# Output weights two groups of value pages later in SyncE's queue, and one value step moved from round 7 to round 58, in a mixed attention decode kernel

## The reference, cut to what matters

```python
def diff_attend(q, k, v, qpos, kpos, lam):
    s = jnp.einsum('bqhcd,bkhcd->bhcqk', q, k).astype(jnp.float32)
    p = masked_softmax(s, kpos[None, :] <= qpos[:, None])
    a = p[:, :, 0] - lam * p[:, :, 1]
    return jnp.einsum('bhqk,bkhv->bqhv', a.astype(v.dtype), v)

def layer_output(x, o_branches, g_n, z_n, o_d, z_d, lam_init, lp):
    ...
    o = jnp.concatenate([o_nsa * jax.nn.silu(z_n), o_d * jax.nn.silu(z_d)], axis=-1)
    return x + o @ lp['w_out']

def sample_layer(x, cache_c, cache_s, cache_dk, cache_dv, win, page_table, lp, lam_init):
    ...
    k_all = jnp.concatenate([gather(cache_dk), k_d], axis=1)
    v_all = jnp.concatenate([gather(cache_dv), v_d], axis=1)
    o_d = diff_attend(q_d, k_all, v_all, pos, jnp.arange(past + T), lam)
```

## Time and profile before

| | us |
|---|---|
| median of 3 runs | 774.43 |
| lowest and highest | 774.13, 775.53 |
| the profiled execution, its own time | 775.79 |
| its span, first to last instruction | 773.9 |
| PE busy in the span | 721.2 |
| DVE busy in the span | 443.2 |

### The profile page before, as it was taken

One profiled execution on the slowest core, in us unless ns is written; L12 is line 12 of the kernel. 1 busy time (PEld: TensorE's weight loads), 2 busy tenths in 40 slices (PEclk: granted clock), 3 DMA queues, 4 the chain that ended last, 5 costly groups with the idle time before them and its releaser, 6 DMA issues.

```text
span 773.9 us, 14663 instructions
## 1 busy us (share of the span) xinstructions
PE 721.2 (93%) x4733; PEld 347.1 (45%) x4733; DVE 443.2 (57%) x953; ACT 200.5 (26%) x529; POOL 104.6 (14%) x198
## 2 busy tenths in 40 slices
PE   6999999999999999999999998888898887999996
PEld 2465544454545365444543562424344352433542
DVE  5351650715531456999768618777769656645373
ACT  3020011101200202311231215535456334433200
POOL 0000000000000010101001665622647000000000
PEclk9999999999999999999999999999999976999999
DMA  8797979899898999987978549999899849984621
GB/s 305 228 320 217 335 231 339 265 385 307 305 345 289 347 334 378 359 311 262 388 236 291 182 154 293 340 330 296 247 326 307 298 150 386 353 282 136 264 118 56
DMA packets 131686, 218.57 MB, mean 282 GB/s; under 512 B 17617, under 2 KB 55738, under 8 KB 130394
## 3 DMA queue, kind: packets, MB, share of 16 engines
q1 hardware_dynamic: 109514, 191.07, 72.1%
q0 software_dynamic: 7456, 14.80, 5.7%
q10 hardware_dynamic: 14640, 11.77, 4.9%
HBM read 211.71 MB, written 10.04 MB: 287 GB/s over the span
## 4 chain that ended last, share of the span: by engine, by line
PE 53%; DVE 16%; issue 11%; SPq 8%; DMA 6%; POOLq 2%; ACT 2%; POOL 1%; DVEq 0%; ACTq 0%
PE banks L634 13%; PE banks L662 9%; SPq L440 7%; PE banks L596 4%; PE banks L1043 4%; PE banks L675 4%; PE banks L762 3%; PE banks L1164 3%; DVE att L1884 3%; DMA proj<-in_cmp_cache 2%; PE banks L981 2%; PE banks L939 2%; PE banks L957 1%; DMA ring<-in_dv_cache 1%; POOLq L454 1%
## 5 line engine op out<-in xcount | busy, mean ns | idle before, releaser
L662 PE MATMUL banks<-ring,xt 128*128 128x512 f32 (+1 forms) x320 | 129.5, 558 | 0.0
L634 PE MATMUL banks<-proj,wide 128*64 128x256 f32 x896 | 98.2, 380 | 1.2 <-DMA proj<-in_cmp_cache 1.2
L1401 ACT ACTIVATE wide<-banks,att 128x384 f32<-128x384 f32 (+3 forms) x128 | 66.3, 523 | 124.5 <-DVE att L1884 121.2
L662 PEld LDWEIGHTS banks<-ring,xt 128*128 128x128 f32 x320 | 59.2, 190 | 63.9 <-issue 61.2
L458 POOL DMA_DIRECT2D ring<-in_sel_cache x143 | 74.8, 523 | 45.4 <-issue 39.1
L634 PEld LDWEIGHTS banks<-proj,wide 128*64 128x64 f32 x896 | 63.7, 137 | 38.0 <-DMA proj<-in_cmp_cache 5.6
L762 PE MATMUL banks<-ring,small 128*32 128x512 f32 x512 | 71.8, 641 | 6.4 <-DMA ring<-in_dv_cache 4.7
L1614 DVE TENSOR_SCALAR small<-small 128x510 f32<-128x510 f32 x8 | 3.4, 426 | 113.7 <-ACT small L1235 97.6
L675 PE MATMUL banks<-ring,small 128*32 128x512 f32 x512 | 61.6, 598 | 2.9 <-DMA ring<-in_dk_cache 2.9
L1883 DVE TENSOR_TENSOR banks<-banks,consts 128x256 f32<-128x256 f32 x64 | 27.3, 427 | 55.7 <-PE banks L939 55.3
L939 PE MATMUL banks<-proj 64*128 64x384 f32 (+7 forms) x256 | 53.5, 496 | 3.5 <-ACT wide L1401 3.5
(11 more groups left out here) (371 smaller groups left out, 883.8 us busy)
## 6 DMA issues: line engine op xcount, KB each, us to landing
ring<-in_dk_cache SPq DMA_DIRECT2D x256, 256.0 KB, 5.7
ring<-in_dv_cache SPq DMA_DIRECT2D x256, 256.0 KB, 5.4
proj<-in_cmp_cache SPq DMA_DIRECT2D x144, 128.0 KB, 2.9
ring<-in_w_in SPq DMA_DIRECT2D x6, 2048.0 KB, 12.5
proj<-in_cmp_cache ACTq DMA_DIRECT2D x80, 128.0 KB, 5.2
ring<-in_sel_cache POOLq DMA_DIRECT2D x143, 32.0 KB, 5.5
ring<-in_cmp_cache SPq DMA_DIRECT2D x32, 128.0 KB, 3.8
ring<-in_w_out SPq DMA_DIRECT2D x2, 2048.0 KB, 11.6
```

The lines of the kernel that those rows point to most:

```text
L634: last = mm(to, w1[:, kv, half, lp, :], rows[:, kv, g, lp, :, :, :], start=lp + half == 0, stop=lp == LP - 1 and half == 1, tile_position= ...
L662: last = mm(banks[:, 3 + n % 2, 0:width(c)], of, by, start=k == 0, stop=k == KC - 1)
L1401: last = A(e_slot(j, c)[:, 0:n], banks[:, 2 * (j % 2) + c, 0:n], ACT.Exp, bias=row_max[:, j % 4, c:c + 1], accum_out=row_sum[:, j % 4, c:c ...
```

## The change

Two numbers change. In `V_NONE` 58 goes out and 7 comes in: round 7 has no V step any more, round 58 has one, and steps 8 to 57 each come one round of the table later (the step is not the same one: what round 8 did for group 9 it now does for group 8). The sums `add_v` of decode rows 1 to 6 move with them. In `W_OUT_AT` 3 is added. Because the table moved too, the first index above round 41 is now 41, so `W_OUT_AT` goes from 44 to 46: in the list of SP each half of `w_out` stands behind two more groups of values.

```diff
-        V_NONE, V_MORE = (2, 32, 37, 40, 44, 58), (13, 16, 54, 61)
+        V_NONE, V_MORE = (2, 7, 32, 37, 40, 44), (13, 16, 54, 61)
...
-        SEL_MORE, W_OUT_AT = 26, V_EARLY + next(v for v in range(64) if v >= V_EARLY and V_ROUNDS[v - V_EARLY] > SEL_AT[1] + 4)
+        SEL_MORE, W_OUT_AT = 26, V_EARLY + 3 + next(v for v in range(64) if v >= V_EARLY and V_ROUNDS[v - V_EARLY] > SEL_AT[1] + 4)
```

## The result

| | before | after |
|---|---|---|
| median of 20 runs, us | 776.75 | 773.01 |
| lowest and highest | 771.68, 781.13 | 769.41, 776.46 |
| span of the profiled execution | 773.9 | 770.9 |
| ratio after / before, 95% interval | | 0.9947 (0.9929 to 0.9964) |

The change makes the kernel faster by 0.53%, 4.1 us, with an interval of 2.8 to 5.5 us. The ratio is that of the means of the runs; the medians lie 3.7 us apart. The median of before over 20 runs lies 2.3 us above the median of the three that were shown first, so sizes are compared by the ratio: forecast 0.9962 (2.9 of 774.4), measured 0.9947. The runs of one kernel spread over 7.1 us (after) and 9.5 us (before). A single profile therefore shows where time went, but its span is no verdict.

What follows compares the result with a forecast made beforehand. PE, busy 93% of the span, was taken as the bound. The terms -0.75 - 0.95 - 1.71 + 0.5 = -2.9 us, from the median 774.43, gave 771.5 us, range 769.2 to 774.8.

Steps and rivals of the forecast that it cites:

- The weights (-0.95 and -1.71): Rounds 45 and 47: PE's waits for value pages behind the two halves of the output weights both go, -0.95 and -1.71 us.
- the likeliest case: Whole kernel: the sum of the terms holds, 771.5 us, chance 0.46.
- rival 2: Slow stretch at steps 46 and 47: PE stays at 2.4 GHz, -1.5 us more, 770.0 us, chance 0.17.
- The narrow place (1.6 us to spare at group 48): Round 50: group 48 lands at 656.1, PE wants it at 657.7, so it is 1.6 us early.
- The weighing of 358 against 387 GB/s: Queue to group 48: at 358 GB/s round 50 would wait 0.1 us; the measured 386 to 387 was used instead.
- The step of round 7 (0 by round 13): Rounds 7 to 13: PE loses 3.14 us of step and waits, but `sel_place` in round 12 stays put, gain 0.
- rival 4: Before round 13: the first half of the selected blocks lands sooner, another -1.2 us, 770.3 us, chance 0.07.
- rival 5: Ahead of round 13's selected scores: PE idles longer, its clock falls, 4.5 us lost, 776.0 us, chance 0.09.
- The sum of decode row 4 (-0.75): Rounds 39 and 40: `add_v` moves ahead of round 40's masks and step 40 finds it done, -0.75 us.
- The other sums (0; round 50's with 0.75 to either side): Five other `add_v` sums, each moved one round later: 0, with 0.75 us to either side for round 49 to 50.
- Round 58 (+0.5): Round 58: the added V step costs +0.5 us, 0.54 of it hidden in the wait for ACT; bounds 0.45 and 1.07.
- three signs of being wrong: `sel_place` moved by over 1 us, a wait for pages at round 50, or slow stretches between 508 and 530.

Runs made afterwards that it cites:

- the weights alone: Kernel before with its old table of V steps and only the output weights moved, 3 added to `W_OUT_AT`: ratio 0.9940, 772.67 us.
- the step alone: Kernel after without the 3 added to `W_OUT_AT`, so only the V step is moved: ratio 0.9992, 776.59 us.
- half-later: Kernel after with the second half of the output weights asked for six groups after the first instead of two: ratio 0.9938, 771.96 us.
- first store-later profile: Kernel after with POOL's two stores of the new values moved behind its selected blocks of the first half: ratio 0.9906, 771.17 us.
- after again: Kernel after run once more, nothing changed: ratio 0.9948, 772.24 us.
- store later again: Second run of kernel after with POOL's two stores of the new values behind its selected blocks of the first half: ratio 0.9931, 772.28 us.
- after with both edits: Kernel after with the weights' second half six groups behind the first and POOL's two stores behind its first-half selected blocks: ratio 0.9899, 769.48 us.
- the halves together: Kernel before with the second half of the output weights directly behind the first, both ahead of group 44: ratio 1.0055, 780.83 us.

## Why the prediction was right, and where it was not

**The weights (-0.95 and -1.71): right in place, too small.** Both waits went, and the weights alone gave the whole gain. The term was 2.66 us; three traces with the weights in the new place on the old table are 3.5 us shorter between rounds 45 and 54, and the ratio makes it 4.7 (0.9940; the interval is 2.2 to 7.1). The 3.5 us have two parts. From the start of round 45's scores to the V step of round 47 it took 15.36 us in both profiles of before and 12.1 to 12.4 in all nine traces with the new place: 3.0 less, for 2.66 of waits. PE's own speed on the way doesn't show in the 15.36: in the second profile of before PE was at the fast clock for longer, waited longer, and reached the step at the same distance. Here are PE and its clock from round 45 to 49 in the two profiles of before and with the weights alone:

```profile
636.62:656.87 20.25, 14.84 (x69) 4.17 (x68) 13.20 (x37) 9.61 (x29) 0.00 (x0) 0.66 1.05 386
...
638.05:658.27 20.22, 13.42 (x69) 4.10 (x68) 13.21 (x37) 9.61 (x29) 0.00 (x0) 0.75 1.05 387
...
635.33:652.04 16.71, 12.85 (x69) 4.07 (x68) 13.21 (x37) 9.63 (x29) 0.00 (x0) 0.80 1.03 375
```

The second part is clock. From that step to round 49, where nothing waits for pages, it took 4.9 us before, 4.3 in the three traces on the old table and in two of the new, and 2.8 in the other four. The second of the late stretches at 1.2 GHz in the earlier trace rows had been left out of the sum as "the clock comes along", and so the term was mis-sized: 0.6 to 2.1 us of it came back. In after the steps of rounds 47 to 49 took 1.06 to 1.07 us each; with the weights alone two of them took 1.36 and 1.74, and in the second profile of after two took 1.94. So the likeliest case and rival 2 are near the ends of what executions do, and the measured gain lies between them.

**The narrow place (1.6 us to spare at group 48): wrong, 1.6 to spare became 2.36 too few.** The two executions are compared from the start of round 38's scores (611.12 before, 612.38 after). The forecast had the group land 45.0 us behind that mark (656.1) and PE come for it 46.6 behind (657.7). It landed 46.66 behind (659.04): 1.7 us late. 0.3 of it is step 41, which ended 19.63 us behind the mark (632.01) and not 0.75 sooner than the 20.07 of before; 0.9 is a term that was left out, from the end of that step to SP's first transfer of group 45 at 632.88; 0.5 is the queue, 26.15 us for a forecast of 25.6. And PE was ready 44.34 us behind the mark (656.72): 2.2 us early. That is the larger part: the forecast took the waits away and left the slow steps of the earlier trace rows in, though it had itself given the clock's coming along a chance. The weighing of 358 against 387 GB/s was right, with 389 measured from 644.1 to 656.7. In the sum the wait costs less than its 2.36, since 0.97 of it stands behind `add_v` anyway. And it is no constant: 2.36, none, 3.30 and 1.87 us in four profiles of kernels with that order. In the profile without it PE came 48.8 us behind the mark, after 10.1 us at 1.2 GHz; in the other three it came after 44.2 to 44.3 us, and the landing, 46.2 to 47.5 us behind the mark, set the length.

**The step of round 7 (0 by round 13): the net was right as far as can be told, the reason not.** The prediction put the landing of the last selected block beyond the reach of the values and gave rival 4 a chance of 0.07. The landings say that it moved: 48.5 us after the start of round 0 in the mean of the five profiles on the old table with the store in its place (49.1, 48.4, 47.9, 49.3, 47.7), 47.2 in the four on the new (46.7, 47.8, 47.9, 46.4). Part of that is clock and not edit: where PE fell to 1.2 GHz in rounds 8 to 10, the last block landed 3.3 to 3.7 us after POOL asked for it, otherwise 4.8 to 5.8. Like compared with like, 47.8 and 47.9 stand against 48.7 in the mean of four without the fall, and 46.7 and 46.4 against 47.7 with it: about 0.8 to 1.1 us sooner. That one group of values less in the queue does this is likely, but not shown apart. The scores of the selected blocks (L1062) came 0.8 us sooner (48.6 against 49.4 in the mean), since in two of the four something else held them: the clock. In the step alone it fell to 1.2 GHz in round 9, in these stretches:

```profile
486.40:489.60 3.20, 1.36 (x11) 0.31 (x5) 3.10 (x8) 3.20 (x11) 1.97 (x5) 1.00 1.07 342
...
489.70:493.00 3.30, 3.30 (x16) 1.64 (x16) 2.85 (x7) 2.29 (x6) 1.85 (x5) 0.50 1.06 340
```

With the V step gone from round 7 and no wait for pages, PE runs up to DVE and ACT, which the first row shows busy for 3.10 and 3.20 of 3.20 us, and stands 0.65 and 1.21 us for them. The half-later and the first store-later profile have the same fall at 488.4 and 490.3; after, after again, store later again and after with both edits have nearly the same idle times and no fall. So round 12 came after 40.4 or after 42.1 to 42.3 us, where the old table had 41.3 to 41.9 and, in the halves together, 43.4. There PE fell too, at 485.5, on a wait of 1.74 us for pages, and stayed slow for 7.5 us: the fall doesn't belong to the moved step alone. It is rival 5's mechanism (PE falls on an idle time), 20 us sooner than it was expected and at 1.7 to 1.9 us rather than 4.5. Between 508 and 528 PE was at 2.4 GHz in every trace, and its idle time ahead of L1062 (0.92 and 1.05 us in the two profiles of after, 1.04 and 0.39 in those of before) did not grow to 1.84 or more, as rival 5 had it. From the start of round 0 to round 38 the four traces on the new table took 148.9 us in the mean and the five on the old 149.5, so the front may have gained some 0.6 us: a gain of about 0.9 us at round 13, less a fall that came in two of four. The forecast of 0 holds in the ratio 0.9992 (0.9963 to 1.0021), which can't tell 0.6 us from nothing. That is in part luck: the landing that was held fixed moved.

**The sum of decode row 4 (-0.75): right on the spot, half of it kept.** PE's step of round 39, the sum ahead of round 40's masks and PE's next small step, in the kernel after, beside the earlier trace rows:

```profile
616.21 1.06 PE L762 MATMUL banks<-ring,small 128*32 128x512 f32 x8
...
618.49 0.75 DVE L1924 TENSOR_SCALAR xt<-banks,att 128x512 f32<-128x512 f32 x1
...
620.04 0.28 PE L1078 MATMUL banks<-small,consts 64*64 64x1 f32 x2 [1.78 <-ACT q_nsa L1473]
```

Step 39 no longer waits. L1078 came 7.66 us after the start of round 38's scores (612.38 to 620.04), before 8.31 (611.12 to 619.43), so 0.65 sooner; PE's wait for ACT grew from 1.29 to 1.78. Over the whole stretch from round 38 to 45 -0.4 us is left, in every trace in which the slow stretch near 619 has its full length (25.0 to 25.1 against 25.3 to 25.9).

**The other sums (0; round 50's with 0.75 to either side): +0.5 in round 50.** PE's wait for it (0.97) is seen only where the pages come in time. One more sum, that of decode row 1, makes PE wait in all seven traces of the new table and in none of the old. In the kernel after:

```profile
521.96 1.07 PE L762 MATMUL banks<-ring,small 128*32 128x512 f32 x8 [0.87 <-DVE xt L1927]
```

It doesn't lengthen its stretch in a way that can be told. On the old table PE waited 0.17 us for such a sum in round 56, and no longer does.

**Round 58 (+0.5): right on the spot, a third of it kept.** From the step of round 57 to the values of round 59 it took 4.80 us before and 5.19 now (688.68 to 693.87), 0.39 more, and the values no longer wait for ACT:

```profile
692.45 1.06 PE L762 MATMUL banks<-ring,small 128*32 128x512 f32 x8
...
693.87 0.87 PE L974 MATMUL banks<-xt,proj 128*64 128x256 f32 x8
```

0.13 us of it is left over rounds 54 to 63 (38.82 against 38.69), the same in every trace without a wait for pages there.

**The sum.** The moved step is -0.4 (row 4), +0.5 (round 50), +0.13 (round 58) and between 0 and -0.6 at the front, so between +0.2 and -0.4, for a forecast of -0.25; the weights are -3.0 up to the step of round 47 and 0.6 to 2.1 of clock behind it, for a forecast of -2.66, less the 0.8 that the new wait of round 50 costs where it stands. The forecast of 0.9962 lies inside the measured interval (0.9929 to 0.9964) at its upper end. What carried the gain, the two waits behind the weights, was named rightly; that the sum comes as close is helped by errors that offset each other. Two of the prediction's three signs of being wrong came all the same: a wait for pages stood at round 50, and `sel_place`, counted from the start of round 0, moved by 1.3 us. Both belong to steps that the sum had at 0 or to spare, and not to the terms that carry it.

What stays open is why the ratio of the weights alone makes it 4.7 us where the traces show 3.5; the interval allows both. Also open is what brings the stretches at 1.2 GHz near 593 and between 740 and 750 us, which come and go in executions of kernels that are the same there. A kernel that takes the sum of decode row 5 out from behind the gates wasn't tried, nor one that fills PE's idle time in round 9.

## What to carry to other kernels

A large load that is needed late should stand in its queue behind as many small loads as its own deadline allows: here its place decided between waits of 6.6 us (both halves ahead of group 44), 2.7 (one half there, one two groups later) and none to 2.4 or, once, 3.3 (two groups later still) for the same bytes. When a queue is reordered, work out the landing of each transfer from the end of the instruction that lets the issuer go on, and the arrival of its user at the fast clock as well as the slow, since a user that no longer waits elsewhere comes sooner. Compare traces by the lengths of stretches between marks and not by absolute times, with at least two profiles of each kernel: the waits of rounds 8 to 10, three rows of the first profile, were not there in the second.

## What the runs showed of the hardware

The granted clock differed between executions of one kernel at the same instructions. Both profiles of after are at 1.2 GHz for 3 to 4 us from round 45's step on; the second is so once more for 10.1 us, from the end of round 47's step on. They took 15.02 and 16.57 us from round 45 to 49, and 18.80 and 19.72 from 49 to 54. In the step alone the fall at 489.7 came behind a stretch in which PE was partly busy (1.36 of 3.2 us) and at no time idle for more than 1.21 us, and with nearly the same idle times (0.64 and 1.21 to 1.26 us) it came in three of seven profiles on the new table. A slow clock ahead of a wait for pages cost nothing: the granted clock was 0.66 and 0.75 from round 45 to 49 in the two profiles of before, and the stretch took 20.25 and 20.22 us. The transfer engines moved 384 to 389 GB/s for this core in the stretches of 3.3 to 12.6 us shown above in which the queue behind the weights was full. The prediction had set 358 GB/s, from the Trainium skill ("DMA: Bandwidth & Descriptors", Bandwidth, Where 436 GB/s comes from), against that. Another page of the Trainium skill ("Perfetto Trace Analysis", Roofline) says that 358 GB/s is the share of a core when both cores of a pair draw on the memory, and that one core alone can go above it, up to what its 16 DMA engines carry. The traces here, of one core, agree with that.
